# Attention scores in clusters, softmax weights transposed two maps at a time, and a new order of the small steps

## The reference

```
xn = RMSNorm(x);  h = xn @ W_in            # 1024 x 2956, split among four mixers
A: stick-breaking attention                 # 4 heads of 64
B: differential attention                   # per head two softmax maps over 32 channels, p1 - lam*p2
C: block-sparse attention                   # at 256 tokens one causal block: softmax over 4 heads of 64
D: compressed + selected + sliding-window   # two of the three branches are causal softmaxes here: 8 maps
merged = sum_i sigmoid(xn @ Wg_i + bg_i) * (o_i @ Wb_i);  x = x + merged @ W_out
x = x + (silu(hn @ W_gate) * (hn @ W_up)) @ W_down,  hn = RMSNorm(x)       # hidden 2816
```

## Time and profile before

| | |
|---|---|
| median of 3 runs | 859.01 us |
| the profiled execution: its own time, its span | 859.28 us, 857.5 us |
| TensorE busy | 851.2 us (99%) |
| VectorE, ScalarE, GpSimd busy | 598.6, 500.4, 267.7 us |
| granted TensorE clock | 9 tenths or more in all 40 slices (mean 1.00) |
| DMA | 155.24 MB, mean 181 GB/s |

### The profile page before, as it was taken

How to read it: one execution, slowest core, us unless ns; L and a number is a source line. 1 busy time by engine, 2 the same in 40 slices (tenths; PEclk the granted TensorE clock), 3 DMA queues, 4 the chain that set the end, 5 groups by cost and what they waited for, 6 DMA issues and landing times.

```text
span 857.5 us, 12229 instructions
## 1 busy us (share of the span) xinstructions
PE 851.2 (99%) x4530; PEld 706.0 (82%) x4530; DVE 598.6 (70%) x932; ACT 500.4 (58%) x837; POOL 267.7 (31%) x253
## 2 busy tenths in 40 slices
PE   9999999999999999999999999999999999999998
PEld 6888887787888888888888788878788888888886
DVE  5566868558868888864555668676587698888552
ACT  6785645676457555553457775556654665556431
POOL 0087714003304444420000967230042144444100
PEclk9999999999999999999999999999999999999999
DMA  9756454445656555565565455454445565565652
GB/s 333 248 156 199 153 189 144 149 146 173 195 170 199 192 183 191 179 206 177 172 212 192 136 194 179 167 172 148 143 159 193 169 213 186 184 188 189 201 193 73
DMA packets 68443, 155.24 MB, mean 181 GB/s; under 512 B 5409, under 2 KB 7841, under 8 KB 68129
## 3 DMA queue, kind: packets, MB, share of 16 engines
q1 hardware_dynamic: 68096, 154.20, 55.4%
q10 hardware_dynamic: 288, 0.27, 0.1%
HBM read 153.40 MB, written 1.05 MB: 180 GB/s over the span
## 4 chain that ended last, share of the span: by engine, by line
PE 96%; DMA 1%; DVE 1%; ACT 1%; issue 0%; SPq 0%; ACTq 0%
PE acc L648 60%; PE acc L637 18%; PE acc L642 9%; PE att L733 2%; PE att L797 1%; PE att L772 1%; PE att L695 1%; PE att L720 1%; DMA w_raw<-in_w_in 1%; PE att L788 1%; PE att L756 0%; DVE xs L1204 0%; DVE w_lo L1135 0%; ACT sq_dump L1010 0%; PE att L810 0%
## 5 line engine op out<-in xcount | busy, mean ns | idle before, releaser
L1135 DVE TENSOR_TENSOR w_lo<-w_raw,w_hi 128x1024 fp32r<-128x1024 f32 (+1 forms) x276 | 357.7, 1307 | 121.4 <-ACT w_hi L905 119.3
L905 ACT ACTIVATE w_hi<-w_raw 128x1024 fp32r<-128x1024 f32 (+1 forms) x275 | 286.5, 1051 | 98.0 <-PE acc L648 69.1
L648 PE MATMUL acc<-w_hi,xt 128*128 128x512 f32 (+1 forms) x1024 | 261.8, 397 | 0.2 <-ACT xt L928 0.2
L648 PEld LDWEIGHTS acc<-w_hi,xt 128*128 128x128 f32 x1024 | 185.5, 188 | 38.9 <-issue 2.2
L637 PE MATMUL acc<-xt,w_hi 128*128 128x512 f32 x704 | 176.8, 393 | 0.5 <-DVE xt L1146 0.5
L1486 POOL TENSOR_TENSOR gate_up<-gate_up,rows 128x256 f32<-128x256 f32 x88 | 107.9, 1245 | 140.4 <-DVE gate_up L1209 122.6
L637 PEld LDWEIGHTS acc<-xt,w_hi 128*128 128x128 f32 x704 | 126.7, 189 | 23.6 <-issue 0.9
L648 PE MATMUL acc<-w_lo,xt 128*128 128x512 f32 (+1 forms) x512 | 136.0, 387 | 0.0
L648 PEld LDWEIGHTS acc<-w_lo,xt 128*128 128x128 f32 x512 | 96.0, 188 | 19.6
L642 PEld LDWEIGHTS acc<-xt,w_lo 128*128 128x128 f32 x704 | 96.0, 190 | 6.9
L642 PE MATMUL acc<-xt,w_lo 128*128 128x256 f32 x704 | 98.1, 282 | 0.0
(11 more groups left out here) (172 smaller groups left out, 815.4 us busy)
## 6 DMA issues: line engine op xcount, KB each, us to landing
w_raw<-in_w_ffn SPq DMA_DIRECT2D x88, 512.0 KB, 4.0
w_raw<-in_w_gate SPq DMA_DIRECT2D x64, 512.0 KB, 3.6
w_raw<-in_w_ffn_down SPq DMA_DIRECT2D x44, 512.0 KB, 4.1
w_raw<-in_w_in SPq DMA_DIRECT2D x39, 512.0 KB, 5.0
w_raw<-in_w_branch SPq DMA_DIRECT2D x16, 512.0 KB, 4.0
w_raw<-in_w_out SPq DMA_DIRECT2D x16, 512.0 KB, 3.5
bg<-in_b_gate SPq DMA_DIRECT2D x8, 512.0 KB, 5.2
w_raw<-in_w_in SPq DMA_DIRECT2D x8, 396.0 KB, 3.4
```

The source lines that it names most:

```text
L648: return pe.matmul(acc[bank0 + t][:, 0:N], x_part[:, k0 + k, t * P:(t + 1) * P], w_part[:, k, 0:N], start=first, stop=last)
L905: act.activation(w_hi[:, n % WR, :, 0:N], w_raw[:, n % RAW, :, 0:N], copy).then_inc(s_hi, 1)
L1135: dve.tensor_tensor(w_lo[:, n % WR, :, 0:N], w_raw[:, n % RAW, :, 0:N], w_hi[:, n % WR, :, 0:N].bitcast(F32), ALU.subtract).then_inc(s_lo, 1)
```

## The change

1. **Slots and ranks.** `PLAN` and `RANK` have new values. Among the ranks, `silu` goes from 4 to 0.5, `f` from 4 to 2.5, `act` from 3.5 to 3, `hid` from 4.5 to 3.5.
2. **Score clusters.** Where `sm` n and `sm` n + 1 (n even) have the same slot, the second (`second(step)`) puts its two maps in the accumulator pair of the next product result (`IDLE`) instead of S0 and S1. In the new plan that holds for B pairs 0 and 1 (slot 21), B pairs 2 and 3 (slot 27), C pairs 0 and 1 (slot 35). Those of B are issued interleaved, four maps in four row groups; those of C pair after pair. The first chunk of that next result waits until VectorE has read the second pair.
3. **Transposes.** C and D: one step `pt` for two maps, six transposes into S0 and S1, one ScalarE copy. B: as before.

```diff
-    "sig": (48, 52, 56, 56), "o": (22, 44, 44, 58), "subln": 36, "prep": (13, 18, 25), "ngate": 25, "Aq": 6,
+    "sig": (51, 56, 57, 57), "o": (22, 45, 43, 58), "subln": 40, "prep": (13, 18, 25), "ngate": 26, "Aq": 6,
...
-    "Bsm": (21, 24, 27, 28), "Bp": (21, 24, 27, 29), "Bpt": (23, 27, 29, 32), "Bpv": (27, 29, 31, 35), "Bo": 36,
-    "Cq": 25, "Ck": 33, "Csm": (35, 36), "Cp": (36, 40), "Cpt": (39, 40, 42, 42), "Cpv": (43, 43), "Dc": 27,
-    "cbuild": 29, "ck": 31, "cks": 31, "cv": 31, "kcprep": 34, "kct": 36, "cr": 35, "cs": 39, "cp": 39,
-    "cpt": 41, "cpv": 45, "Dq": 34, "Dk": 38, "Dsm": (40, 42, 46, 52), "Dp": (41, 42, 47, 52),
-    "Dpt": (43, 45, 47, 50, 51, 53, 55, 56), "Dpv": (46, 55, 55, 57),
+    "Bsm": (21, 21, 27, 27), "Bp": (21, 23, 27, 30), "Bpt": (23, 27, 30, 34), "Bpv": (25, 29, 33, 35), "Bo": 39,
+    "Cq": 26, "Ck": 33, "Csm": (35, 35), "Cp": (35, 38), "Cpt": (39, 40), "Cpv": (41, 41), "Dc": 27,
+    "cbuild": 28, "ck": 31, "cks": 32, "cv": 32, "kcprep": 33, "kct": 34, "cr": 36, "cs": 38, "cp": 40,
+    "cpt": 42, "cpv": 45, "Dq": 33, "Dk": 40, "Dsm": (41, 42, 46, 48), "Dp": (41, 42, 47, 51),
+    "Dpt": (45, 47, 51, 53), "Dpv": (46, 52, 52, 54),
...
-    "x0": 0, "f0": 0, "m0": 0, "proj": 4, "zg": 4.5, "merge": 0.5, "xadd": 0.5, "act": 3.5, "silu": 4, "hid": 4.5, "split": 5, "rows": 1, "Acum": 5.5,
-    "Dp": 6, "cpv": 6, "sig": 4.5, "Cpv": 3, "cbuild": 1.5, "kct": 4.5, "x": 0.5, "Asp": 6, "Bpv": 4.5, "ck": 1,
-    "cv": 1.5, "cs": 3.5, "prep": 0.5, "Csm": 3, "Dpv": 4.5, "lambda": 2.5, "stats": 1.5, "subln": 6, "Bsm": 4,
-    "Bpt": 6, "ngate": 1.5, "Cp": 5, "kcprep": 2, "f": 4, "Bp": 5.5,
+    "x0": 0, "f0": 0, "m0": 0, "proj": 4, "zg": 5.5, "merge": 0.5, "xadd": 2.5, "act": 3, "silu": 0.5,
+    "hid": 3.5, "split": 5, "rows": 2.5, "Acum": 5.5, "Dp": 4, "cpv": 6, "sig": 5.5, "Cpv": 3, "cbuild": 1,
+    "kct": 5, "x": 0.5, "Asp": 5.5, "Bpv": 1, "ck": 1, "cv": 5, "cs": 3.5, "prep": 0.5, "Csm": 3, "Dpv": 1.5,
+    "lambda": 2, "stats": 1.5, "subln": 4.5, "Bsm": 4, "Bpt": 6, "ngate": 4.5, "Cp": 5, "kcprep": 2, "f": 2.5,
+    "Bp": 4.5,
...
+def second(step):
+    kind, a = step
+    return kind == "sm" and a[1] % 2 == 1 and PLAN[a[0] + "sm"][a[1]] == PLAN[a[0] + "sm"][a[1] - 1]
...
+IDLE_USES = [s for s in ORDER if second(s)]
+IDLE_OF = {s: RESULTS[result_at(SLOT[s]) + 1] for s in IDLE_USES}
...
+                for s in IDLE_USES if first else ():
+                    if IDLE_OF[s] == step:
+                        pe.wait_ge(read_dve.sem, read_dve.at(l, s))
...
+            def score_matmuls(l, todo, swap=False):
+
+                for t in (0, 1) if swap else (1, 0):
+                    for step, n, buf, (r, q, k) in todo:
+                        still, move, c0, c1, at = (k, q, t * P, 2 * P, 2 * P * t) if swap else (q, k, 0, (t + 1) * P, t * P)
+                        mm = pe.matmul(score_bank(l, step, n)[:, at:at + c1 - c0], qkt[buf][r, still, t * P:(t + 1) * P],
+                                       qkt[buf][r, move, c0:c1], start=not swap and t == 1, stop=t == (1 if swap else 0),
+                                       skip_group_check=True)
+                        if t == (1 if swap else 0) and n == 1:
+                            mm.then_inc(att_done.now(step), 1)
...
+                if mixer == "B":
+                    score_matmuls(l, sum(todo, []))
+                else:
+                    for maps in todo:
+                        score_matmuls(l, maps, swap=kind == "z")
...
-                    e = 2 * (m % 2) if mixer == "B" else m % 4
-                    pe.wait_ge(dve_misc.sem, dve_misc.at(l, ("p", (mixer, pair_of(mixer, m)))))
-                    for s in range(3):
-                        mm = pe.transpose(att[:, TP, s * P:(s + 1) * P], eb[:, e, s * P:(s + 1) * P], ident)
+                    maps = [(TP, 2 * (m % 2))] if mixer == "B" else [(S0 + i, 2 * (m % 2) + i) for i in range(2)]
+                    pe.wait_ge(dve_misc.sem, dve_misc.at(l, ("p", (mixer, m))))
+                    for b, e in maps:
+                        for s in range(3):
+                            mm = pe.transpose(att[:, b, s * P:(s + 1) * P], eb[:, e, s * P:(s + 1) * P], ident)
...
-                    act.activation(ptb[:, pb, :], att[:, TP, 0:384], copy).then_inc(read_act.now(step), 1)
+                    dst, src = ((ptb[:, pb, :], att[:, TP, 0:384]) if a[0] == "B"
+                                else (ptb[:, pb:pb + 2, :], att[:, S0:S0 + 2, 0:384]))
+                    act.activation(dst, src, copy).then_inc(read_act.now(step), 1)
```

More of the change, by code:

```diff
@@ L151, in steps @@
             put(PLAN["prep"]["BCD".index(mixer)], "prep", mixer)
+        for n in range(PAIRS[mixer] if mixer != "A" else 0):
+            put(PLAN[mixer + "sm"][n], "sm", (mixer, n))
         for n in range(PAIRS[mixer]):
-            for kind in {"A": ("z", "sp", "cum", "pv"), "B": ("sm", "p")}.get(mixer, ("sm", "p", "pv")):
+            for kind in {"A": ("z", "sp", "cum", "pv"), "B": ("p",)}.get(mixer, ("p", "pv")):
                 put(PLAN[mixer + kind][n], kind, n if mixer == "A" and kind != "pv" else (mixer, n))
@@ L239, in now, with result_at @@
         return self.sem
-TP, OB, S0, S1 = range(4)
+TP, OB, S0, S1, IDLE = range(5)
+def second(step):
+    kind, a = step
+    return kind == "sm" and a[1] % 2 == 1 and PLAN[a[0] + "sm"][a[1]] == PLAN[a[0] + "sm"][a[1] - 1]
+SLOT = {s: u for u in range(NCH + 1) for s in STEPS[u]}
+def result_at(u):
+    kind, a, b = CHUNKS[u]
+    return RESULTS.index({"in": ("proj", a), "gate": ("zg", a)}[kind])
+IDLE_USES = [s for s in ORDER if second(s)]
+IDLE_OF = {s: RESULTS[result_at(SLOT[s]) + 1] for s in IDLE_USES}
 def banks_of(step):
     kind, a = step
+    if kind == "pt" and a[0] != "B":
+        return (S0, S1)
     if kind == "pair":
@@ L253, in banks_of @@
         return (TP,)
+    if second(step):
+        return (IDLE,)
     if kind in ("z", "cum", "sm", "cs"):
@@ L290, in pt_slots @@
     kind, a = step
-    return (2 * a, 2 * a + 1) if kind == "cum" else (a[1] % 4,)
+    if kind == "pt" and a[0] == "B":
+        return (a[1] % 4,)
+    n = a if kind == "cum" else a[1] % 2
+    return 2 * n, 2 * n + 1
 PT_USES = [[s for s in ORDER if s[0] in ("cum", "pt") and slot in pt_slots(s)] for slot in range(4)]
@@ L301, in pv_step @@
     mixer, m = s[1]
-    return ("pv", (mixer, m if mixer == "B" else m // 2))
+    return ("pv", (mixer, m))
 def trunk_kernel(nc, x, x_t, w_in, w_gate, w_branch, w_out, w_ffn, w_ffn_down,
@@ L513, in e_free, with score_bank @@
                     engine.wait_ge(att_done.sem, att_done.at(prev[0], e_of(prev[1])[1]))
+        def score_bank(l, step, i):
+            return acc[bank_pair(l, IDLE_OF[step]) + i] if second(step) else att[:, S0 + i, :]
         block = ctx.enter_context(nc.Block())
@@ L589, in bank_free @@
                 for b in banks_of(step):
+                    if b == IDLE:
+                        n = RESULTS.index(IDLE_OF[step]) - 2
+                        before = RESULTS[n]
+                        ev = proj_out if before[0] == "proj" else dve_acc
+                        pe.wait_ge(ev.sem, ev.at(l, before))
+                        if IDLE_USES.index(step):
+                            before = IDLE_USES[IDLE_USES.index(step) - 1]
+                            pe.wait_ge(read_dve.sem, read_dve.at(l, before))
+                        continue
                     prev = previous(l, BANK_USES[b], step)
@@ L721, in qk @@
                 mm.then_inc(att_done.now(step), 1)
[L723 to L734, removed]
+            def score_matmuls(l, todo, swap=False):
[4 more added lines that the diff above has]
+                                       qkt[buf][r, move, c0:c1], start=not swap and t == 1, stop=t == (1 if swap else 0),
                                        skip_group_check=True)
-                return mm
+                        if t == (1 if swap else 0) and n == 1:
+                            mm.then_inc(att_done.now(step), 1)
             def scores(l, step):
                 kind, a = step
-                bank_free(l, step)
+                if second(step):
+                    return
                 mixer, n = ("A", a) if kind == "z" else a
+                group = [step] + [s for s in IDLE_USES if kind == "sm" and s[1] == (mixer, n + 1)]
+                for s in group:
+                    bank_free(l, s)
                 if n == 0:
@@ L745, in scores @@
                         pe.wait_ge(s_mask16, 1)
-                buf, maps = maps_of(mixer, n)
-                mm = causal(buf, maps, swap=mixer == "A")
-                mm.then_inc(att_done.now(step), 1)
+                todo = []
+                for s in group:
+                    buf, maps = maps_of(mixer, s[1] if kind == "z" else s[1][1])
+                    todo.append([(s, i, buf, m) for i, m in enumerate(maps)])
+                if kind == "z":
+                    for b in (S0, S1):
```

(4 more changed lines are left out.)

10 lines of the change are left out of this document (4 added, 6 removed).

## The result

The changed kernel takes 860.29 us (median, 859.89 to 860.70), the kernel before, run on the same chips, 858.94 us (858.59 to 859.47). The ratio is 1.0015, with a 95% interval of 1.0008 to 1.0021: slower by 1.35 us, where +6.3 was forecast. The time lies in the range given, but the size of the change is less than a quarter of what was worked out, and it lies inside the 0.2% that I had counted as no change.

The account below looks back on a forecast made before the run. TensorE's own instruction stream was taken to bound the kernel. Per layer, attention -1.84, ffn start -0.43 and ffn ring +5.4, times two, gave +6.3 us: 865.3 us predicted, range 857 to 869.5.

Parts of the forecast that it names:

- What bounds the kernel, and the sign: Whole program: TensorE's own instruction stream sets the time; the change makes it slower (chance 0.77), by 6.3 us.
- The ring's links and its length: Ffn: GpSimd product, `silu`, hi split, lo split, `act`, next product take 5.96 us; TensorE needs 5.59 per group.
- The ring's head start: Ffn: 1.29 us in hand at group 4, gone after four groups; 18 x 0.37 - 1.29 = 5.4 us lost per layer.
- B's clusters: Attention, B's scores: four maps run at once, a cluster costing a pair and 0.02 more; 2.16 us saved per layer.
- pair behind pair: Rival for B's clusters: second pair follows the first, 0.64 longer per cluster, 2.6 us more, 867.9; chance 0.06.
- The compressed branch: Attention: `ck` in slot 31 and `cv` in 32 each pay the change into small groups and back; 0.43 us lost per layer.
- Waits through TP: Attention: Dq waits for Ck's copy in slot 33 (0.94 lost), B's last transposes for `kct` in slot 34 (0.33), per layer.
- The sum of attention: Attention: savings and losses of its six items add up to -1.84 us per layer.
- C's scores: Attention: second pair follows the first at 0.64 instead of a second entry at 0.86 to 1.10; 0.40 us saved per layer.
- the transposes: Attention, C and D: steps of six instead of two of three save 0.30 us per layer; slot 42's idle 0.58 goes.
- the neighbours: Attention: other steps come to share slots or lose a neighbour; 0.1 us saved per layer.
- The ffn's start: Start of ffn: copies of the new x go ahead of a split, TensorE's wait for the lo part goes; -0.43 us per layer.

Follow-up runs that it names:

- experiment 1: Changed kernel with the old ranks of `silu` (4), `act` (3.5) and `hid` (4.5): 853.89 us, ratio 0.9938.
- experiment 2: Kernel before with only the rank of `silu` changed, 4 to 0.5: 865.58 us, ratio 1.0074.
- experiment 3: Changed kernel with `act` rank 3 to 2.9, ahead of the split, `silu` still at 0.5: 855.21 us, ratio 0.9954.
- experiment 4: Changed kernel with GpSimd scaling only the gate half of each group, the up half's factor left out: 853.88 us, ratio 0.9938.
- experiment 5: Changed kernel with `silu` at old rank 4 in groups 0 to 10, new rank 0.5 only in groups 11 to 21: 853.61 us, ratio 0.9944.
- experiment 6: Changed kernel with `silu` at old rank 4 in groups 11 to 21, new rank 0.5 only in groups 0 to 10: 853.83 us, ratio 0.9942.
- experiment 7: Kernel of experiment 1 with B's clusters issued pair behind pair instead of four maps interleaved: 853.63 us, ratio 0.9939.
- experiment 11: Kernel of experiment 9 with `cv` in slot 31 at rank 1.5, directly behind `ck`: 851.65 us, ratio 0.9913.
- experiment 8: Kernel of experiment 1 with step Ck moved from slot 33 to 31: 851.88 us, ratio 0.9919.
- experiment 9: Kernel of experiment 8 with `kct` moved from slot 34 to 35, rank 5 to 2.9, ahead of the split: 851.53 us, ratio 0.9912.
- experiment 10: Kernel of experiment 9 but `kct` in slot 35 keeps its old rank 5, behind the split: 853.64 us, ratio 0.9940.
- experiment 12: Kernel before with only the rank of `f` changed, 4 to 2.5: 857.84 us, ratio 0.9987.

## Why the prediction was wrong

*What bounds the kernel, and the sign.* Right. TensorE's own stream sets the time, the attention part gets shorter, and a ring closed by one rank costs more than that gives (experiments 1 and 2).

*The ring's links and its length.* Right: 5.93 us measured, 5.96 forecast; experiments 3 and 4 each brought it under 5.59 at another link.

*The ring's head start.* This step failed: "So 1.29 us in hand, gone after four groups." I let the ring run at its full 5.96 us from GpSimd's product 1 on, with 2.53 us for that product, its length in the kernel before. In the changed kernel the first two that count last 1.43 and 1.73 us, and the starts behind them are 4.83 and 5.13 us apart. That is 1.11 + 0.81 = 1.92 us less than at full length, all of it lead. VectorE's split beside product 1 and GpSimd's product 2 in the kernel before, then ScalarE's and VectorE's rows ahead of and beside product 1 in the changed kernel:

```profile
262.14 1.21 DVE L1135 TENSOR_TENSOR w_lo<-w_raw,w_hi 128x1024 fp32r<-128x1024 f32 x1
266.66 1.73 POOL L1486 TENSOR_TENSOR gate_up<-gate_up,rows 128x256 f32<-128x256 f32 x2 [1.83 <-DVE gate_up L1209]
...
257.40 1.28 ACT L1043 ACT_TABLE_LOAD   x1
258.69 0.42 ACT L1043 ACTIVATE silu<-gate_up 128x256 f32<-128x256 f32 x1
...
260.10 1.71 DVE L1187 TENSOR_TENSOR w_lo<-w_raw,w_hi 128x1024 fp32r<-128x1024 f32 x1 [0.88 <-ACT w_hi L955]
```

Before, a lo split started 0.16 us ahead of product 1: the split took 1.21 us and the product 2.53. In the new order that split's hi part stands on ScalarE behind `silu` 0, and `silu` 0 behind a table load of 1.28 us, so the lo split starts 0.80 us into the product; then the product takes 1.43 and the split 1.71. With the old order back (experiment 1), product 1 takes 2.54 again. Product 2 lasts 1.73 in either order: that row of the kernel before I had not used. My reading "beside an idle VectorE" was not right either: beside that first product of 1.44 us a lo split ran from 259.87 on, for 1.68 us.

With this lead, and 0.02 us less per group, 5.4 becomes 5.4 - 1.9 - 0.4 = 3.1; measured 3.25. Experiments 5 and 6 show the same from the other side: the ring's pace in one half of the groups costs nothing in the second half, and 0.14 us per layer in the first. The sentence "TensorE idle ahead of every second chunk from group 8 on" was wrong for that reason; it is group 13. For the program this is 4.3 us of the 5.0 by which the forecast was too high.

*B's clusters.* Right, and the sum for them holds: no time beyond that of one pair. The bound that I kept (pair behind pair, 2.6 us more) rested on a wrong picture: the order of issue doesn't decide it (experiment 7). By the Trainium skill's figure ("TensorE: Matmul & The Clock Gate", Measured speedup vs the span model) the cluster would have been some 0.2 us longer than a pair, by the prediction's estimate; this trace does not agree, as the chunk that holds it took 3.23 us for 3.21.

*The compressed branch.* +0.43 per layer was too much, and put on the wrong step. Where `cv` stands makes no difference (experiment 11). What costs is that `cks`, which followed `cv` directly before, has left for slot 32, and pays the entry there with or without `cv`. TensorE's timeline of the kernel before, from the earlier trace rows on:

```profile
107.53 0.27 PE L857 MATMUL att<-kpart,cst 128*16 128x64 f32 x2
107.73 0.88 PE L788 MATMUL att<-proj,ptb 128*128 128x64 f32 x6
108.42 2.09 PE L648 MATMUL acc<-w_hi,xt 128*128 128x512 f32 x8
```

That chunk with its slot took 4.80; less a plain chunk and the 0.69 of B's products, 1.39. After the change the two chunks take 3.52 + 3.60, less two plain ones 1.68. So 0.29 lost (an estimate from these rows) and not 0.43. As forecast, the change adds one way into small groups and out again; but it falls to the slot of `cks`, with or without `cv`, and it is cheaper. Whether `cks` back in slot 31 would save the 0.29 was not tested.

*Waits through TP.* Ck to Dq 0.94, right (experiment 8: 2.0 us for two layers). `kct` 0.33: the wait is there, but only 0.15 per layer was had back, since in slot 35 both ranks that were tried bring a wait of their own (experiments 9 and 10).

*The sum of attention.* -1.84 against -2.07 and -2.10. With 0.29 for the compressed branch the forecast would have been -1.98; the 0.1 left over, among C's scores, the transposes and the neighbours, was not told apart.

*The ffn's start.* -0.43 against -0.50 (experiment 12).

*The start of the program*, 0.43 us in this profile, is in no step; the medians do not show it.

## What to carry to other kernels

When an order closes a ring that is longer than the work it feeds, its cost is (groups x excess) less the lead, and the lead needs the same care as the period: walk the first turns with what each engine has beside it in the new order, not with durations from the old one. Engines in strict order can leave few free places: one transposing step moved by two slots gave back all of its wait, while one small copy, moved once ahead of a split and once behind it, made a new wait both times. Price the way into small row or column groups per place on TensorE's stream, not per step.

## What the runs showed of the hardware

- Matmuls in row groups that are free start ahead of earlier ones whose row groups are busy: the second pair's start 20 ns behind the first pair's, though the first pair's two 128-column matmuls (four records), which stood ahead of them, started 0.5 us later (experiment 7). Two pairs that share their row groups start 0.75 us apart (C in experiment 9). The Trainium skill ("TensorE: Matmul & The Clock Gate", The mechanism) says that matmuls start and end strictly in program order, and only weight loads are pulled ahead; this trace shows otherwise for the starts of matmuls in different row groups. Whoever lets one semaphore on the last matmul stand for all of them should look at this.
- Matmuls of two steps in different column groups run side by side without being issued as one run: `cks` uses 16 columns of the first group, `cv` all four groups of 32, and three of `cv`'s records start at 108.09, between those of `cks` at 108.08 and 108.14 (experiment 9).
- The same two multiplications on GpSimd take 1.43, 1.73 or 2.53 us in one and the same kernel, and VectorE's lo split 1.21 to 1.77. It goes by which started first: a split that started 0.16 us ahead of the product took 1.21 and the product 2.53 (the kernel before), one that started 0.80 us into it took 1.71 and the product 1.43. One that starts 0.17 us into it (334.71 behind 334.54) makes both long, 1.77 and 2.53: the product is two multiplications, and the second comes up behind the split.
